# Transposing each expert tile on VectorE in two operations of 1024 columns instead of four of 512

## The chip, the core and the metric

One core of a Trainium2 chip runs the whole program. The metric is the time of one execution in microseconds (us), as the device measures it. The engines of the core run side by side, each with its own instruction stream, and meet at semaphores: TensorE (PE, with PEld for its weight loads), VectorE (DVE), ScalarE (ACT), GpSimd (POOL) and SyncE (SP), which here only starts transfers from HBM.

## What is computed

One transformer-like layer over 256 tokens of width 2048: a mixing part (projections, gated linear attention and retention, output projection, layer norm), and then an expert part. The change lies in the expert part alone, whose first half is this, cut from the reference:

```python
q = (xt @ w_q).reshape(t, PEER_HEADS, 2, PEER_QDIM // 2)
scores = jnp.einsum('thpd,hpkd->thpk', q, subkeys)
vals, idx = lax.top_k(scores, PEER_TOPK)          # then 16 of the 16 x 16 sums, and a softmax of them
...
act = gelu(einsum('tkd,td->tk', u_tab[eb], xb))   # u_tab: 16384 experts x 2048
out = einsum('tk,tkd->td', gates * act, v_tab[eb])
```

The kernel doesn't gather the rows of `u_tab`. It multiplies all 16384 experts with all tokens, applies the gelu, and weights the result by a matrix that holds the gates of the chosen experts and zero elsewhere. Products of float32 are made from two parts of each operand, an upper and a lower one in a rounded 32-bit format, so that each tile of `u_tab` needs an upper part, a lower part, and two matmuls.

## The kernel before

**The U stage.** `u_tab` is taken in 128 tiles of 128 experts by 2048 columns (1 MB each). A tile must be turned, so that its columns lie on the partitions. It is loaded so that transposing blocks of 32 by 32 is enough. A tile is worked in four quarters of 512 columns, and each quarter goes through four engines:

- SyncE loads the tile into a buffer `u_raw` with four transfers (`load_u`, L341). There are two such buffers, three for tiles 6 to 47. A load waits until `ut_done` tells that the last tile in its buffer is wholly transposed.
- VectorE transposes a quarter from `u_raw` into one of the six slots of the ring `u_t` (L907, in `u_quarter`). It waits until the transfer has landed (`u_in`, at the first quarter) and until TensorE has finished the quarter that lay in the slot six quarters earlier (`uparts_free`).
- ScalarE copies the quarter to its upper part `u_hi` (L547), after `ut_done`.
- GpSimd subtracts and gives the lower part `u_lo` (L1201), after `uhi_done`.
- TensorE waits for `ulo_done` and runs eight matmuls in four pairs: `u_hi` with 512 columns (L1469) and `u_lo` with 256 (L1470). Then it counts `uparts_free` up.

`u_hi` and `u_lo` lie in rings of the same six slots. `slot(j, f)` is `(4 * j + f) % 6`: quarter `f` of tile `j`, tiles counted in sixes. Quarters are numbered 0 to 511 below; the quarter `n` needs the slot of `n - 6`.

**What else VectorE does between the quarters.** Its order is written out by hand. For every tile two behind, `u_add` (L995) adds two halves of the sum before the gelu. In tiles 0 to 23 pieces of the search for the best keys are put behind the second and the fourth quarter (`route_best`, two tiles of three; its stage 3 is L929 and L933, in tiles 4 and 16). In tiles 25 to 50 come the pieces of `route_pick`, one for each tile. From tile 64 on, each tile also has `spread` (L1044), `weigh` (L1052), `hot_rows` (L1030) and `hot_cols` (L1036, four operations), in `u_spread_tile`. `hot_rows` and `hot_cols` make the two operands of four products (L1451) that TensorE runs behind the first quarter of the same tile, once `hot_done` tells of them.

**Behind the U stage** the same scheme runs with the table V, where nothing is transposed: TensorE's matmuls are L1509, and VectorE makes the lower parts (L1090, L1094).

Of the kernel before, what the change touches and what calls it, by code (L numbers as in the profile page):

```python
# [53 lines left out]
U_TWO = 48  # L54
# [39 lines left out]
def build(nc, x, w_in, w_up, b_gate, gla_g, ret_g, w_out, ln1_g, ln1_b, w_q, subkeys, peer_u, peer_v,  # L94
          ln2_g, ln2_b, keep_c, mix_c, out):
    ctx = ExitStack()
    with ctx:
# [6 lines left out]
        def at(name, off, shape, dt=F32):  # L104
            return nc.alloc_sbuf_tensor_at(name, shape, dt, offset=base + off)
# [51 lines left out]
        u_raw = [at(f"u_raw{s}", off, [P, 4 * COL]) for s, off in enumerate((WRK, WRK + 8 * K, BIG + 64 * K))]  # L157
        u_t = at("u_t", WRK + 16 * K, [P, UR, 4 * P])
# [63 lines left out]
        def slot(j, f):  # L222
            return (4 * j + f) % UR
# [20 lines left out]
        ut_done, uhi_done, ulo_done, uparts_free, gelu_done, gelu_free = (  # L244
            sem(n) for n in ("ut_done", "uhi_done", "ulo_done", "uparts_free", "gelu_done", "gelu_free"))
# [420 lines left out]
        def _(dve):  # L666
# [226 lines left out]

            def u_quarter(ii, j, f, three=False):
                s = j % 3 if three else j % 2
                if f == 0:
                    if three:
                        before = 2 * (ii - 1) + j // 3 + 3 * (s < 2)  # L900
                    elif isinstance(ii, int) and ii == 0:
                        before = j // 2
                    else:
                        before = (ii - U_TWO // 6) * 3 + j // 2 + 3 + (U_TWO - 6) // 3
                    dve.wait_ge(u_in[s], before * 64 + 64)
                dve.wait_ge(uparts_free, ii * 24 + 4 * j + f + 1)
                dve.transpose(u_t[:, slot(j, f), :].rearrange("p (f b l) -> p b f l", f=4, b=4),  # L907
                              u_raw[s][:].rearrange("p (b f l) -> p b f l", b=4, l=32)[:, :, 4 * f:4 * f + 4, :]).then_inc(ut_done, 1)


            def route_best(stage, part):
# [38 lines left out]
            def route_split():  # L950


                dve.drain()
                dve.tensor_copy(gmax[:], tops[:, :, 0])
                dve.tensor_copy(idx_f[:].rearrange("p a h s k -> p (a h s k)"), idx_u[:].rearrange("p a r k -> p (a r k)"))
                dve.tensor_scalar(sel_ab[:, 0], sel_u[:], 4, None, ALU.logical_shift_right)
                dve.tensor_scalar(sel_ab[:, 1], sel_u[:], 15, None, ALU.bitwise_and)
                dve.drain()
                dve.tensor_tensor(tops[:], tops[:], gmax[:].unsqueeze(2).to_broadcast([P, TT * PH, TOPK]), ALU.subtract).then_inc(soft_d, 1)
                dve.tensor_copy(sel_f[:], sel_ab[:])  # L960

            def route_pick(s, a, stage, part):

                h0 = 4 * part
                p4 = pick.rearrange("p (h k) a -> p h k a", h=4)
                dve.drain()
                if stage == 0:
                    dve.wait_ge(iota_done, 1)
                    dve.tensor_tensor(pick, iota_ps[:, 0:TOPK].unsqueeze(1).to_broadcast([P, 4 * TOPK, TOPK]),
                                      sel_f[:, s, a * PH + h0:a * PH + h0 + 4].rearrange("p n k -> p (n k)").unsqueeze(2).to_broadcast([P, 4 * TOPK, TOPK]),  # L970
                                      ALU.is_equal)
                elif stage == 1:
                    dve.tensor_tensor(p4, p4, idx_f[:, a, h0:h0 + 4, s, :].unsqueeze(2).to_broadcast([P, 4, TOPK, TOPK]), ALU.mult)
                else:
                    dve.tensor_reduce(ijg[:, s, a, h0 * TOPK:(h0 + 4) * TOPK], pick, AX.X, ALU.add).then_inc(ijg_done, 1)

            def route_gates():
                dve.wait_ge(soft_e, 1)
                dve.drain()
                dve.tensor_reduce(gmax[:], tops[:], AX.X, ALU.add)  # L980
                dve.drain()
                dve.reciprocal(rstd[:], gmax[:])
                dve.drain()
                dve.tensor_tensor(ijg[:, 2].rearrange("p a (h k) -> p (a h) k", k=TOPK), tops[:],
                                  rstd[:].unsqueeze(2).to_broadcast([P, TT * PH, TOPK]), ALU.mult).then_inc(ijg_done, 1)
# [5 lines left out]
            def u_add(ii, j, late=0):  # L991

                dve.wait_ge(cross_done, ii * 6 + j + 1)
                z = u_bank(j)[:, 0:T]
                dve.tensor_tensor(z, z, cross_sb[late][:], ALU.add).then_inc(u_sum, 1)  # L995

            for i in range(U_TURN // 6 * 6):
                for f in range(4):
                    u_quarter(i // 6, i % 6, f, three=6 <= i < U_TWO)
                    if i > 1 and f == 2:  # L1000
                        u_add(i // 6, i % 6 - 2)
                    if i < 24 and i % 3 < 2 and f % 2:
                        n = i // 3 * 2 + i % 3
                        route_best(n % 8, 4 * (f // 2) + 2 + n // 8)
                    elif U_PICK <= i and f == 1:
                        n = i - U_PICK
                        route_pick(n // 12, n // 6 % 2, n % 3, n // 3 % 2)
                if i == 24:
                    route_split()
                elif i == 30:  # L1010
                    route_gates()
            route_pick(1, 1, 2, 1)
            with dve.Fori(U_TURN // 6, U_SPREAD // 6) as ii:
                for j in range(6):
                    for f in range(4):
                        u_quarter(ii, j, f)
                        if f == 2:
                            u_add(ii, j - 2, 1)
            for i in range(U_SPREAD // 6 * 6, U_SPREAD):
                for f in range(4):  # L1020
                    u_quarter(i // 6, i % 6, f)
                    if f == 2:
                        u_add(i // 6, i % 6 - 2, 1)


            def hot_rows(q):

                if not isinstance(q, int) or q:
                    dve.wait_ge(spread_mm, q)
                dve.tensor_tensor(hot_j[:], iota.unsqueeze(1).to_broadcast([P, 4, P]),  # L1030
                                  bank(4)[:, bass.ds(T + q * 4, 4)].unsqueeze(2).to_broadcast([P, 4, P]), ALU.is_equal)

            def hot_cols(q):
                for k in range(4):
                    t = bass.ds(q * 4 + k, 1)
                    ins = dve.tensor_scalar(hot_i[:, k, :], iota_ps, pick_ig[:, 0, t], pick_ig[:, 1, t], ALU.is_equal, ALU.mult)  # L1036
                ins.then_inc(hot_done, 1)

            def spread(q, r):

                dve.drain()
                dve.wait_ge(spread_mm, q + 1)
                g4 = act_w[:, :, bass.ds(q, 1)].rearrange("p h q i t -> p h (q i) t")
                dve.tensor_tensor(g4, g4, bank(2 + r).rearrange("p (t h i) -> p h i t", t=4, h=2), ALU.mult).then_inc(spread_free, 1)  # L1044

            def weigh(ii, j):

                i = ii * 6 + j
                dve.drain()
                dve.wait_ge(gelu_done, i + 1)  # L1050
                w = tile_w(1, i - P // 2)
                dve.tensor_tensor(w, w, by_four(u_bank(j)[:, 0:T]), ALU.mult).then_inc(gelu_free, 1)  # L1052

            def u_spread_tile(ii, j, spreads=True, weighs=True):
                q = ii * 6 + j - U_SPREAD
                u_quarter(ii, j, 0)
                if spreads:
                    spread(q - 2, j % 2)
                u_quarter(ii, j, 1)
                if weighs:  # L1060
                    weigh(ii, j - 3)
                u_quarter(ii, j, 2)
                u_add(ii, j - 2, 1)
                hot_rows(q)
                u_quarter(ii, j, 3)
                hot_cols(q)

            dve.wait_ge(ijg_sb, 1)
            for i in range(U_SPREAD, U_UNROLL):
                if i == U_SPREAD + 2:  # L1070
                    dve.wait_ge(ones_done, 16)
                    dve.wait_ge(gelu_done, U_SPREAD)
                u_spread_tile(i // 6, i % 6, spreads=i > U_SPREAD + 1, weighs=i > U_SPREAD + 2)
            with dve.Fori(U_UNROLL // 6, P // 6) as ii:
                for j in range(6):
                    u_spread_tile(ii, j)
            for j in range(2):
                u_spread_tile(P // 6, j)
# [491 lines left out]
```

## Time and profile before

| | us |
|---|---|
| median of 3 runs | 2061.8 |
| the runs | 2057.56, 2061.80, 2062.09 |
| profiled execution | 2061.78 |
| its span in the profile | 2060.0 |
| TensorE busy | 2028.4 |
| VectorE busy | 1231.1 |
| ScalarE busy | 970.8 |
| GpSimd busy | 1089.0 |

The span is the time from the first instruction to the last; 1.8 us of the profiled execution lie around it. The U stage runs from about 569 us (first matmul of L1469) to about 1348 us. The times in the rows below are counted from the span's start.

### The profile page before, as it was taken

To read this page: it belongs to the slowest core of one execution; us is meant where nothing else is said; L and a number is where in the kernel's file an instruction comes from. 1 tells how busy PE (TensorE), PEld (TensorE's weight loads), DVE (VectorE), ACT (ScalarE), POOL (GpSimd) and SP (SyncE) were. 2 spreads that over 40 slices of the span, in tenths; PEclk is the share of its full clock that TensorE was granted. 3 is DMA by queue.
4 is the path that set the end of the run, shared out by engine and by line. 5 is a ranking of instruction groups with operands and counts; after the bars stand their busy time and mean duration, and the time that the engine had idled before them with its cause. 6 is when DMAs were issued, how large, how long until landed. Compare 5 with 4: busy or idle time off the path is not lost.

```text
span 2060.0 us, 34135 instructions
## 1 busy us (share of the span) xinstructions
PE 2028.4 (98%) x11230; PEld 1763.3 (86%) x11230; DVE 1231.1 (60%) x2147; ACT 970.8 (47%) x1436; POOL 1089.0 (53%) x699
## 2 busy tenths in 40 slices
PE   8999999999999999999999999999999999999997
PEld 8998888878988888888888888888888888888885
DVE  1753121123878877658899999955555555555557
ACT  4544334444455566574444444444444444444442
POOL 6877778886778998898777777700000000000000
PEclk9999999999999999999999999999999999999998
DMA  8555657576678887676666666665555555555553
GB/s 281 174 153 167 195 176 248 179 201 170 166 170 192 192 190 186 163 185 164 164 163 163 163 163 163 164 262 186 199 188 196 191 192 195 189 198 186 201 185 140
DMA packets 149282, 381.29 MB, mean 185 GB/s; under 512 B 15568, under 2 KB 18256, under 8 KB 131424
## 3 DMA queue, kind: packets, MB, share of 16 engines
q1 hardware_dynamic: 149072, 380.27, 64.0%
q8 instruction: 42, 0.69, 0.1%
q14 instruction: 24, 0.20, 0.0%
q10 hardware_dynamic: 144, 0.13, 0.0%
HBM read 376.15 MB, written 4.19 MB: 185 GB/s over the span
## 4 chain that ended last, share of the span: by engine, by line
PE 88%; POOL 5%; issue 4%; DVE 1%; DMA 1%; DVEq 1%; ACT 0%; SPq 0%; POOLq 0%; ACTq 0%
PE ps L1509 33%; PE ps L1469 20%; PE ps L1470 10%; PE ps L1228 6%; PE ps L1230 6%; PE ps L1229 6%; PE ps L1451 3%; POOL w_lo L1162 3%; POOL u_lo L1201 2%; DMA raw<-in_w_in 1%; PE ps L1325 1%; DVEq L655 0%; PE ps L1434 0%; DVE h_again L656 0%; PE ps L1343 0%
## 5 line engine op out<-in xcount | busy, mean ns | idle before, releaser
L1469 PE MATMUL ps<-xT,u_hi 128*128 128x512 f32 x2048 | 727.5, 399 | 0.4 <-POOL u_lo L1201 0.4
L1201 POOL TENSOR_TENSOR u_lo<-u_t,u_hi 128x512 fp32r<-128x512 f32 x512 | 653.1, 1297 | 129.2 <-ACT u_hi L547 126.9
L1470 PE MATMUL ps<-xT,u_lo 128*128 128x256 f32 x2048 | 573.3, 280 | 0.0
L547 ACT ACTIVATE u_hi<-u_t 128x512 fp32r<-128x512 f32 x512 | 321.0, 632 | 359.9 <-DVE u_t L907 358.6
L1162 POOL TENSOR_TENSOR w_lo<-raw,w_hi 128x1024 fp32r<-128x1024 f32 x175 | 427.3, 2457 | 119.1 <-ACT w_hi L404 115.5
L1469 PEld LDWEIGHTS ps<-xT,u_hi 128*128 128x128 f32 x2048 | 384.7, 188 | 90.8 <-POOL u_lo L1201 0.5
L907 DVE STREAM_TRANSPOSE u_t<-u_raw 128x512 f32<-128x512 f32 x512 | 356.4, 703 | 105.5 <-PE ps L1470 75.5
L1470 PEld LDWEIGHTS ps<-xT,u_lo 128*128 128x128 f32 x2048 | 386.7, 189 | 0.0
L1167 POOL TENSOR_TENSOR small<-small 128x1 f32<-128x1 f32 x4 | 2.8, 699 | 707.6 <-DVE small L1122 707.6
L1509 PE MATMUL ps<-v_hi,m_hi 128*128 128x512 f32 x1024 | 316.6, 389 | 0.0
L1509 PE MATMUL ps<-v_lo,m_hi 128*128 128x512 f32 x1024 | 316.6, 389 | 0.0
L1509 PE MATMUL ps<-v_hi,m_lo 128*128 128x512 f32 x1024 | 316.6, 389 | 0.0
L404 ACT ACTIVATE w_hi<-raw 128x1024 fp32r<-128x1024 f32 x175 | 184.7, 1059 | 274.8 <-PE ps L1230 263.7
L1090 DVE TENSOR_TENSOR v_lo<-v_raw,v_hi 128x1024 fp32r<-128x1024 f32 x128 | 156.8, 1225 | 141.8 <-ACT v_hi L622 141.8
L1509 PEld LDWEIGHTS ps<-v_hi,m_lo 128*128 128x128 f32 x1024 | 192.2, 188 | 39.9
L1509 PEld LDWEIGHTS ps<-v_lo,m_hi 128*128 128x128 f32 x1024 | 192.2, 188 | 39.9
L1509 PEld LDWEIGHTS ps<-v_hi,m_hi 128*128 128x128 f32 x1024 | 192.1, 188 | 39.9
L622 ACT ACTIVATE v_hi<-v_raw 128x1024 fp32r<-128x1024 f32 x126 | 133.7, 1061 | 164.6 <-PE ps L1509 148.0
L1228 PE MATMUL ps<-xT,w_hi 128*128 128x256 f32 x640 | 183.9, 287 | 2.3 <-DVE xT L662 1.8
L1094 DVE TENSOR_TENSOR v_lo<-v_raw,v_hi 128x1024 fp32r<-128x1024 f32 x128 | 156.8, 1225 | 48.4 <-ACT v_hi L627 48.4
L1229 PE MATMUL ps<-xT,w_hi 128*128 128x256 f32 x640 | 181.6, 284 | 0.0
L1230 PE MATMUL ps<-xT,w_lo 128*128 128x256 f32 x640 | 181.5, 284 | 0.0
(191 smaller groups left out, 2313.0 us busy)
## 6 DMA issues: line engine op xcount, KB each, us to landing
u_raw<-in_peer_u SPq DMA_DIRECT2D x512, 256.0 KB, 4.8
v_raw<-in_peer_v SPq DMA_DIRECT2D x128, 1024.0 KB, 4.8
raw<-in_w_in SPq DMA_DIRECT2D x111, 512.0 KB, 3.7
raw<-in_w_out SPq DMA_DIRECT2D x32, 512.0 KB, 3.7
raw<-in_w_peer_q SPq DMA_DIRECT2D x128, 128.0 KB, 3.5
x_again<-in_x SPq DMA_DIRECT2D x1, 2048.0 KB, 9.0
h_dram<-o_sb SPq DMA_DIRECT2D x1, 2048.0 KB, 8.4
h_again<-h_dram SPq DMA_DIRECT2D x1, 2048.0 KB, 12.6
```

Source lines behind the costliest of these rows:

```text
L404: act.activation(w_hi[:, k % HI_RING, :], raw[:, k, :], ACT.Copy).then_inc(hi_done, 1)
L547: act.activation(u_hi[:, slot(j, f), :], u_t[:, slot(j, f), :], ACT.Copy).then_inc(uhi_done, 1)
L907: dve.transpose(u_t[:, slot(j, f), :].rearrange("p (f b l) -> p b f l", f=4, b=4), u_raw[s][:].rearrange("p (b f l) -> p b f l", b=4, l=32 ...
L1090: dve.tensor_tensor(v_lo[:, 2 * s, :], v_raw[:, 2 * s, :], vh[0].bitcast(F32), ALU.subtract)
L1162: pool.tensor_tensor(w_lo[:, k, :], raw[:, k, :], w_hi[:, k % HI_RING, :].bitcast(F32), ALU.subtract).then_inc(lo_done, 1)
L1201: pool.tensor_tensor(u_lo[:, r, :], u_t[:, r, :], u_hi[:, r, :].bitcast(F32), ALU.subtract).then_inc(ulo_done, 1)
L1228: pe.matmul(o, lh, rh, start=start, stop=False, skip_group_check=lint)
L1229: pe.matmul(o, lh, rl, start=False, stop=False, skip_group_check=lint)
L1230: return pe.matmul(o, ll, rh, start=False, stop=stop, skip_group_check=lint)
L1469: pe.matmul(acc, u_hi[:, r, c], xT[:, :, kt, :], start=kt == 0, stop=False)
L1470: ins = pe.matmul(acc[:, 0:T], u_lo[:, r, c], xT_hi[:, kt, :], start=False, stop=kt == KT - 1)
L1509: ins = pe.matmul(bank(4 * a + 2 * h + c), m, v[:, c * 512:(c + 1) * 512], start=start and p == 0, stop=stop and p == 2)
```

## The change

The four transposes of a tile become two. `u_quarter` becomes `u_half`: one operation turns 1024 columns (two quarters) into two slots of the ring that lie side by side, and counts `ut_done` up by two. It waits until both slots are free, so for the count of its second quarter. The first half takes the place of quarter 0 in VectorE's order, the second that of quarter 2. ScalarE, GpSimd and TensorE keep their code: they still work quarter by quarter, with the same counts.

```diff
-            def u_quarter(ii, j, f, three=False):
+            def u_half(ii, j, f, three=False):
...
-                dve.wait_ge(uparts_free, ii * 24 + 4 * j + f + 1)
-                dve.transpose(u_t[:, slot(j, f), :].rearrange("p (f b l) -> p b f l", f=4, b=4),
-                              u_raw[s][:].rearrange("p (b f l) -> p b f l", b=4, l=32)[:, :, 4 * f:4 * f + 4, :]).then_inc(ut_done, 1)
+                dve.wait_ge(uparts_free, ii * 24 + 4 * j + f + 2)
+                r = slot(j, f)
+                dve.transpose(u_t[:, r:r + 2, :].rearrange("p f n -> p (f n)").rearrange("p (f b l) -> p b f l", f=8, b=4),
+                              u_raw[s][:].rearrange("p (b f l) -> p b f l", b=4, l=32)[:, :, 4 * f:4 * f + 8, :]).then_inc(ut_done, 2)
...
             for i in range(U_TURN // 6 * 6):
                 for f in range(4):
-                    u_quarter(i // 6, i % 6, f, three=6 <= i < U_TWO)
+                    if f % 2 == 0:
+                        u_half(i // 6, i % 6, f, three=6 <= i < U_TWO)
...
             def u_spread_tile(ii, j, spreads=True, weighs=True):
                 q = ii * 6 + j - U_SPREAD
-                u_quarter(ii, j, 0)
+                u_half(ii, j, 0)
                 if spreads:
                     spread(q - 2, j % 2)
-                u_quarter(ii, j, 1)
                 if weighs:
                     weigh(ii, j - 3)
-                u_quarter(ii, j, 2)
+                u_half(ii, j, 2)
                 u_add(ii, j - 2, 1)
                 hot_rows(q)
-                u_quarter(ii, j, 3)
                 hot_cols(q)
```

VectorE's rows in tile 4, where stage 3 of the search lies between the quarters (`u_raw_95` is the buffer of this tile, `u_raw_96` that of tile 5). Before:

```order
L907 STREAM_TRANSPOSE u_t<-u_raw_95 128x4x4x32 [waits uparts_free,u_in0]
L907 STREAM_TRANSPOSE u_t<-u_raw_95 128x4x4x32 [waits uparts_free]
L929 MAX_INDEX idx_u<-vals,scores 128x8 x4
L933 TENSOR_TENSOR cand<-vals 128x256 x2
L907 STREAM_TRANSPOSE u_t<-u_raw_95 128x4x4x32 [waits uparts_free]
L995 TENSOR_TENSOR ps<-ps,cross_early 128x256 [waits cross_done]
L907 STREAM_TRANSPOSE u_t<-u_raw_95 128x4x4x32 [waits uparts_free]
L929 MAX_INDEX idx_u<-vals,scores 128x8 x4
L933 TENSOR_TENSOR cand<-vals 128x256 x2
L907 STREAM_TRANSPOSE u_t<-u_raw_96 128x4x4x32 [waits uparts_free,u_in1]
```

Now (lines behind L907 are one higher):

```order
L908 STREAM_TRANSPOSE u_t<-u_raw_95 128x4x8x32 [waits uparts_free,u_in0]
L930 MAX_INDEX idx_u<-vals,scores 128x8 x4
L934 TENSOR_TENSOR cand<-vals 128x256 x2
L908 STREAM_TRANSPOSE u_t<-u_raw_95 128x4x8x32 [waits uparts_free]
L996 TENSOR_TENSOR ps<-ps,cross_early 128x256 [waits cross_done]
L930 MAX_INDEX idx_u<-vals,scores 128x8 x4
L934 TENSOR_TENSOR cand<-vals 128x256 x2
L908 STREAM_TRANSPOSE u_t<-u_raw_96 128x4x8x32 [waits uparts_free,u_in1]
```

The fourth quarter has moved ahead of `u_add`, and the first quarter of tile 5 is no longer ready before its second.

VectorE's rows at the end of a tile from 64 on, between its third quarter and `hot_cols`. Before:

```order
L907 STREAM_TRANSPOSE u_t<-u_raw_96 128x4x4x32 [waits uparts_free]
L993 REGISTER_ALU
L995 TENSOR_TENSOR ps<-ps,cross_late 128x256 [waits cross_done]
L1029 REGISTER_ALU
L1030 ISA [waits spread_mm]
L1030 TENSOR_TENSOR hot_j<-keepc,ps 128x512
L906 REGISTER_ALU
L907 STREAM_TRANSPOSE u_t<-u_raw_96 128x4x4x32 [waits uparts_free]
L1036 ISA
L1036 TENSOR_SCALAR hot_i<-ps,pick_ig 128x128
```

Now:

```order
L908 STREAM_TRANSPOSE u_t<-u_raw_96 128x4x8x32 [waits uparts_free]
L994 REGISTER_ALU
L996 TENSOR_TENSOR ps<-ps,cross_late 128x256 [waits cross_done]
L1033 REGISTER_ALU
L1034 ISA [waits spread_mm]
L1034 TENSOR_TENSOR hot_j<-keepc,ps 128x512
L1040 ISA
L1040 TENSOR_SCALAR hot_i<-ps,pick_ig 128x128
```

The wait for the slot of quarter 3 now stands ahead of `u_add` and `hot_rows`, which before ran while VectorE would have waited for that slot.

## Rows read from the trace of the kernel before

**Rows 1.** The page: busy time by engine, and TensorE's share in 40 slices.

```profile
PE 2028.4 (98%) x11230; PEld 1763.3 (86%) x11230; DVE 1231.1 (60%) x2147; ACT 970.8 (47%) x1436; POOL 1089.0 (53%) x699
...
PE   8999999999999999999999999999999999999997
```

**Rows 2.** The page's groups: line engine operation xcount | busy us, mean ns | idle before.

```profile
L1469 PE MATMUL ps<-xT,u_hi 128*128 128x512 f32 x2048 | 727.5, 399 | 0.4 <-POOL u_lo L1201 0.4
L1201 POOL TENSOR_TENSOR u_lo<-u_t,u_hi 128x512 fp32r<-128x512 f32 x512 | 653.1, 1297 | 129.2 <-ACT u_hi L547 126.9
...
L907 DVE STREAM_TRANSPOSE u_t<-u_raw 128x512 f32<-128x512 f32 x512 | 356.4, 703 | 105.5 <-PE ps L1470 75.5
...
L1090 DVE TENSOR_TENSOR v_lo<-v_raw,v_hi 128x1024 fp32r<-128x1024 f32 x128 | 156.8, 1225 | 141.8 <-ACT v_hi L622 141.8
```

**Rows 3.** Window 668 to 930: length, TensorE busy (instructions), clock, DMA share, GB/s.

```profile
668.00:930.00 262.00, 262.00 (x1487) 1.00 0.77 183
```

**Rows 4.** Timeline, TensorE, 595 to 668: start us, us, engine, line, operation.

```profile
595.70 0.40 PE L1469 MATMUL ps<-xT,u_hi 128*128 128x512 f32 x1
...
598.47 0.40 PE L1469 MATMUL ps<-xT,u_hi 128*128 128x512 f32 x1
...
599.15 0.47 PE L1469 MATMUL ps<-xT,u_hi 128*128 128x512 f32 x1 [0.17 <-POOL u_lo L1201]
...
600.63 0.40 PE L1469 MATMUL ps<-xT,u_hi 128*128 128x512 f32 x1
...
606.30 0.40 PE L1469 MATMUL ps<-xT,u_hi 128*128 128x512 f32 x1
...
666.72 0.40 PE L1469 MATMUL ps<-xT,u_hi 128*128 128x512 f32 x1
...
667.43 0.50 PE L1469 MATMUL ps<-xT,u_hi 128*128 128x512 f32 x1 [0.20 <-POOL u_lo L1201]
```

**Rows 5.** Timeline, VectorE, tiles 4 and 5, and tile 17's first quarters.

```profile
587.32 1.32 DVE L907 STREAM_TRANSPOSE u_t<-u_raw 128x512 f32<-128x512 f32 x2 [0.49 <-DMA u_raw<-in_peer_u]
...
591.74 0.70 DVE L907 STREAM_TRANSPOSE u_t<-u_raw 128x512 f32<-128x512 f32 x1
...
594.67 1.67 DVE L933 TENSOR_TENSOR cand<-vals 128x256 f32<-128x256 f32 x2
596.27 1.88 DVE L907 STREAM_TRANSPOSE u_t<-u_raw 128x512 f32<-128x512 f32 x3
...
664.64 1.88 DVE L907 STREAM_TRANSPOSE u_t<-u_raw 128x512 f32<-128x512 f32 x3
```

**Rows 6.** Timeline, ScalarE and GpSimd, tile 5.

```profile
597.00 1.23 ACT L547 ACTIVATE u_hi<-u_t 128x512 fp32r<-128x512 f32 x2 [2.70 <-DVE u_t L907]
...
597.71 5.06 POOL L1201 TENSOR_TENSOR u_lo<-u_t,u_hi 128x512 fp32r<-128x512 f32 x4 [1.98 <-ACT u_hi L547]
```

**Rows 7.** Timeline, tiles 59 and 60: VectorE, then GpSimd, then TensorE.

```profile
903.00 0.71 DVE L907 STREAM_TRANSPOSE u_t<-u_raw 128x512 f32<-128x512 f32 x1 [0.33 <-PE ps L1470]
905.64 1.31 DVE L907 STREAM_TRANSPOSE u_t<-u_raw 128x512 f32<-128x512 f32 x2 [1.92 <-DMA u_raw<-in_peer_u]
...
901.49 5.06 POOL L1201 TENSOR_TENSOR u_lo<-u_t,u_hi 128x512 fp32r<-128x512 f32 x4 [0.58 <-ACT u_hi L547]
...
905.63 0.40 PE L1469 MATMUL ps<-xT,u_hi 128*128 128x512 f32 x1
```

**Rows 8.** Timeline, tiles 66 and 67: VectorE, then TensorE.

```profile
944.24 0.71 DVE L907 STREAM_TRANSPOSE u_t<-u_raw 128x512 f32<-128x512 f32 x1 [0.48 <-PE ps L1470]
944.87 1.32 DVE L1036 TENSOR_SCALAR hot_i<-ps,pick_ig 128x128 f32<-128x128 f32 x4
...
949.27 0.40 DVE L995 TENSOR_TENSOR ps<-ps,cross_late 128x256 f32<-128x256 f32 x1
949.58 0.67 DVE L1030 TENSOR_TENSOR hot_j<-keepc,ps 128x512 f32<-128x512 f32 x1
...
948.20 1.05 PE L1451 MATMUL ps<-hot_i,hot_j 128*128 128x128 f32 x8
```

More of the change, by code:

```diff
@@ L1015, in _ @@
                     for f in range(4):
-                        u_quarter(ii, j, f)
+                        if f % 2 == 0:
+                            u_half(ii, j, f)
                         if f == 2:
@@ L1020, in _ @@
                 for f in range(4):
-                    u_quarter(i // 6, i % 6, f)
+                    if f % 2 == 0:
+                        u_half(i // 6, i % 6, f)
                     if f == 2:
```

## The prediction

> **What bounds the kernel now.** I read the page first. TensorE is busy 98% of the span and its digits stand at 9 in every slice behind the first, while VectorE has 60% [rows 1]. So a saving on VectorE counts only where TensorE is waiting for it. The groups of the page say how often that is in the U stage: before its 2048 matmuls of L1469 TensorE was idle for 0.4 us in all, and GpSimd's `u_lo` ended that [rows 2]. A window over tiles 17 to 63 shows it busy all the time at the full clock, 2.4 GHz [rows 3]. "Busy" hides a short wait, because the ends of matmuls are modelled, so I then went by the starts. A pair (L1469 and L1470) takes 0.346 us between 595.70 and 598.47 (eight pairs in 2.77 us). The start at 599.15 comes 0.68 us after the one before it, so TensorE lost 0.33 us there; the start at 667.43 comes 0.71 us after 666.72, a loss of 0.36 us against the 0.354 us of that stretch [rows 4]. Both times the profile names GpSimd. They are the first quarters of tile 5 (number 20) and tile 17 (number 68). These 0.7 us are all that the U stage loses to its feed, out of some 780 us.
>
> **Why it waits in those two places.** The chain to a quarter is transpose, upper part, lower part, matmuls, and the ring of six slots lets it run up to six quarters ahead. In tiles 4 and 16 the search puts some 3 us of other work between transposes, twice. In tile 4 the transposes start at 587.32 (two), 591.74, and, for quarter 20, at 596.27, right behind L933 [rows 5]. ScalarE takes quarter 20 at 597.00, GpSimd at 597.71 [rows 6], and with 1.30 us for the lower part [rows 2] it is ready at 599.01, when TensorE has run dry. Tile 17 repeats this from 664.64 on [rows 5].
>
> **What the change removes, adds and moves.**
>
> *The transpose itself.* Before, 512 operations of 0.703 us, less their overlap: two in a row take 1.32 us [rows 2, 5]. The trace has no transpose of 1024 columns. From above it is bounded by two of 512 in a row, 1.32 us. From below by the nearest VectorE operation of 1024 columns, L1090 with 1.225 us [rows 2]. I take 1.24 us: L1090 is the row of the same length, and one operation should not cost more than that class by much. VectorE then saves 0.08 us a pair, or 256 x 0.08 = 20 us of its busy time. None of it lies on the path, except in the two waits above, so it is worth 0.7 us at the very most.
>
> For the same term the Trainium skill (Vector Engine (DVE) Microarchitecture Reference, section 5.2) gives 1.0417 ns a column plus about 75 ns an instruction; by that, as an estimate, a merged pair would take 1.14 us and the saving would be 46 us of VectorE's time. The sum for the kernel would be the same, since what hides it is TensorE's own work. The Trainium skill (VectorE: DVE Perf Modes, section on the TRN2 errata) advises few large tiles because the latency is exposed between instructions; no row here shows VectorE's throughput as the bound, so I give that advice no weight against what follows.
>
> *The first quarter of a pair comes out later.* It now waits for the second quarter's slot too, and for the whole operation: 1.24 us instead of 0.70. In the two dry places I count it through. Tile 4's first pair must wait for the slot of quarter 17, which comes free when TensorE starts quarter 12: without its stall TensorE would have started quarter 20 at 598.82 (599.15 less 0.33), and quarter 12 eight steps of 4 x 0.346 us before, 587.75. The wait of VectorE ends about 0.2 us behind such a start. So the pair begins at 587.95 instead of 587.32, ends 0.55 us later than before, and the search behind it moves by as much. In front of the second piece the pair 18, 19 and `u_add` save some 0.1 us. The search therefore ends at 596.7, against 596.27. Then the pair 20, 21 ends at 597.95, where quarter 20 alone ended at 596.97. GpSimd starts and ends some 0.95 us later, and TensorE starts quarter 20 at 600.1 instead of 599.15: **+0.9 us**. In tile 17 the same pattern of instructions gives the same shift, since TensorE too is 0.9 us later by then, and with it the slots: **+0.9 us** again.
>
> Below, this is bounded by 0.54 us each (the longer operation alone), above by 1.95 us each (a whole quarter less in the ring, 1.41 us, plus 0.54). So the term is +1.8 us, between +1.1 and +3.9.
>
> *The usual tile.* In tiles 59 and 60 GpSimd has the first quarter of tile 59 ready at 902.8 (901.49 plus 1.29), and TensorE starts it at 905.63: a margin of 2.8 us [rows 7]. The change takes 0.5 to 1.4 us of it. GpSimd is the tightest of the helpers, with 4 x 1.27 us in a tile of 5.66 us, and has 0.58 us idle ahead of each tile [rows 7]. Its idle time moves but need not grow. Cost: nothing. What hides it is the ring; without that cover each tile would lose up to 0.54 us.
>
> *The transfers.* SyncE's next load waits for the whole tile to be transposed. The last pair starts where quarter 3 started, for the same slot (903.00 in tile 59), and ends 0.53 us later. The next tile's pair would be later by that at its transfer, but it waits for quarter 1's slot anyway, which before was served 0.65 us behind quarter 0. VectorE's 1.9 us of idle time before 905.64 is such a wait for a transfer [rows 7]. Cost: nothing, out of the same 2.8 us.
>
> *From tile 64 on.* `hot_cols` now stands behind the pair, `u_add` and `hot_rows`, all of which wait for the slot of quarter 3. In tile 66 that slot came at 944.24, `hot_cols` ended at 946.19, and TensorE began the four products at 948.20: a margin of 2.0 us [rows 8]. Now it ends at 944.24 + 1.24 + 0.31 (949.27 to 949.58) + 0.67 + 1.32 = 947.78. That leaves **0.4 us**, and I count nothing, but this is the thinnest cover that the change leaves, and 64 tiles stand behind it.
>
> **The sum.** 2061.78 (the profiled execution; it equals the median to 0.02 us, so nothing is added for the difference) + 1.8 = **2063.6 us**.
>
> **The rivals.**
>
> 1. *The pitch after a wait.* After the stall at 599.15 the pairs come every 0.354 us (sixteen pairs from 600.63 to 606.30), before it every 0.346 us [rows 4]. The clock is the same. So TensorE falls into one of at least two rhythms when it starts again after a wait, and in this run both restarts led into the slow one. Other start times may lead into the fast one. Between tiles 17 and 50 there are 34 x 16 = 544 pairs, worth 544 x 0.008 = 4.3 us; with tiles 5 to 16 and 51 to 63 it is 7.2 us. Against it: two of two restarts in the trace were slow. For it: the same trace shows the fast one in the same code, and one of the three runs of before took 4.2 us less than the others. Time: 2059.3, down to 2056.4.
>
> 2. *More dry places.* Tiles 4 and 16 are not the only ones where VectorE does other work. If each further heavy tile starts a quarter poorer, up to three more of them (pieces of the search, and the one-time work behind tiles 24 and 30) run dry, at 0.9 to 1.95 us each: 2064.5 to 2069.4. Against it: the whole window from 668 to 930 shows no idle TensorE today [rows 3].
>
> 3. *Slower, in the last 64 tiles.* TensorE waits for `hot_done`. It decides at 0.4 us: were the operation, or a wait of `u_add` for ScalarE, longer by more than that, each of 64 tiles would lose the excess. With 0.6 us too much it is 64 x 0.2 = 12.8 us, or 2076.4. For it: the margin is a fifth of what it was. Against it: all the terms are from rows of this very stretch, and `u_add` waited for nothing there.
>
> 4. *VectorE's saved time reaches the path.* The dry places come because VectorE is late, and each pair gives back 0.08 us or more. Then both stalls go: 2061.1. Against it: a pair gives its first quarter 0.54 us later, which is far more than it saves.
>
> That the change isn't made as it says is ruled out: VectorE's rows show one transpose where two stood.
>
> **Chances and range.** The forecast 0.50, rival 1 0.27, rival 2 0.12, rival 3 0.05, rival 4 0.06. A measurement of this kernel tells a change from none at about 0.3%, here 6.2 us, so "same" is 2055.6 to 2068.0. The forecast, nearly all of rivals 1 and 4 and two thirds of rival 2 lie in it: 0.87. Faster 0.04, the far end of rival 1; slower 0.09, the end of rival 2 and rival 3. The range leaves out rival 3 and both far ends: 2057.0 to 2067.5.
>
> **What the next profile would show.** VectorE: 256 transposes of 128x1024 near 1.24 us, its busy time near 1210 us. TensorE: the starts of quarters 20 and 68 each some 0.9 us later than one pair behind the start before, beyond today's stall; nothing of that kind elsewhere up to tile 63. The four products of L1451 start on time, some 0.4 us after `hot_cols` ends. The pitch behind the two restarts tells rival 1 from the forecast. Wrong I would be if VectorE's pair took well over 1.32 us, if TensorE's digits fell below 9 in the U stage, or if a stage without transposes changed its length.

## The result and the profile after

| | before | changed |
|---|---|---|
| median, us | 2059.41 (7 runs) | 2067.37 (7 runs) |
| lowest and highest | 2057.56, 2062.09 | 2065.93, 2069.47 |
| profiled execution, its span | 2061.78, 2060.0 | 2067.37, 2064.5 |
| first to last matmul of L1469 (now L1471) | 569.2 to 1348.0 | 569.4 to 1352.5 |

The ratio is 1.0038, with an interval of 1.0029 to 1.0047. The change makes the kernel slower, by 8.0 us. The forecast was 2063.6 us, 1.8 us over the profiled execution of before, and 0.87 had been put on "within 0.3%". The time lies inside the range, 0.1 us from its upper end; the ratio, 1.0038, lies outside the 0.3%.

The page after, against [rows 1, 2]: VectorE has 20 us less to do, just as worked out, and TensorE waits ten times as long before `u_lo`. The columns of a group are those of [rows 2].

```profile
span 2064.5 us, 33942 instructions
...
PE 2029.8 (98%) x11230; PEld 1766.5 (86%) x11230; DVE 1211.3 (59%) x1891; ACT 945.9 (46%) x1436; POOL 1086.8 (53%) x699
...
L1471 PE MATMUL ps<-xT,u_hi 128*128 128x512 f32 x2048 | 727.2, 399 | 4.5 <-POOL u_lo L1203 4.3
...
L908 DVE STREAM_TRANSPOSE u_t<-u_raw 128x1024 f32<-128x1024 f32 x256 | 317.6, 1241 | 134.1 <-PE ps L1472 110.9
```

A transpose of 1024 columns takes 1.241 us. The idle time of L1471 was 0.4 us [rows 2] and is 4.5. 4.3 us of it are three waits, of quarters 20, 68 and 100 (TensorE's timeline after, as [rows 4]):

```profile
601.47 0.47 PE L1471 MATMUL ps<-xT,u_hi 128*128 128x512 f32 x1 [1.88 <-POOL u_lo L1203]
...
671.73 0.63 PE L1471 MATMUL ps<-xT,u_hi 128*128 128x512 f32 x1 [1.78 <-POOL u_lo L1203]
...
718.59 0.50 PE L1471 MATMUL ps<-xT,u_hi 128*128 128x512 f32 x1 [0.64 <-POOL u_lo L1203]
```

From start to start, less the 0.35 us of a pair, TensorE loses 2.05, 1.95 and 0.80 us there. Two more waits are too short for the idle column: quarters 18 and 66 start 0.60 and 0.64 us behind the start before them, a loss of 0.25 and 0.29. Together 5.3 us, against 0.7 before.

How VectorE fares in tiles 4 and 5 after (to be laid beside [rows 5]), and GpSimd below it:

```profile
588.25 1.25 DVE L908 STREAM_TRANSPOSE u_t<-u_raw 128x1024 f32<-128x1024 f32 x1 [0.29 <-DMA u_raw<-in_peer_u]
...
590.92 2.32 DVE L934 TENSOR_TENSOR cand<-vals 128x256 f32<-128x256 f32 x2
593.17 1.23 DVE L908 STREAM_TRANSPOSE u_t<-u_raw 128x1024 f32<-128x1024 f32 x1
594.33 0.40 DVE L996 TENSOR_TENSOR ps<-ps,cross_early 128x256 f32<-128x256 f32 x1
...
596.04 2.12 DVE L934 TENSOR_TENSOR cand<-vals 128x256 f32<-128x256 f32 x2
598.08 2.36 DVE L908 STREAM_TRANSPOSE u_t<-u_raw 128x1024 f32<-128x1024 f32 x2
```

```profile
590.24 2.73 POOL L1203 TENSOR_TENSOR u_lo<-u_t,u_hi 128x512 fp32r<-128x512 f32 x2 [0.27 <-ACT u_hi L547]
595.14 2.73 POOL L1203 TENSOR_TENSOR u_lo<-u_t,u_hi 128x512 fp32r<-128x512 f32 x2 [2.18 <-ACT u_hi L547]
600.05 2.52 POOL L1203 TENSOR_TENSOR u_lo<-u_t,u_hi 128x512 fp32r<-128x512 f32 x2 [2.18 <-ACT u_hi L547]
```

The two sums of a piece take 2.32 and 2.12 us, where before they took 1.86 and 1.67 (the second is the 1.67 of [rows 5]). Each time GpSimd is at work on the two quarters of the pair just turned, and its two operations take 2.73 us instead of the 2.52 of the pair at 600.05, beside which no sums run. Taken one by one, the four sums of tile 4 took 0.43, 1.52, 1.34 and 0.41 us before, so in each piece one of the two met GpSimd; after, they take 0.89, 1.51, 0.69 and 1.51 us, so both do.

Behind quarter 68 something else shows. Windows after, VectorE to GpSimd left in (columns: TensorE, weight loads, VectorE, ScalarE and GpSimd busy, then granted clock, DMA share, GB/s):

```profile
671.73:675.40 3.67, 3.67 (x12) 3.08 (x13) 1.74 (x3) 2.11 (x5) 3.67 (x4) 0.54 0.83 209
```

For 3.7 us the granted clock is 0.54, so near the lower of TensorE's two levels, 1.2 GHz. The clock was at full speed up to a wait of 1.95 us; 4.9 us earlier there had been a wait of 0.29 us. A pair takes 0.64 us there, which costs 1.6 us more.

**Where the 8.0 us are.** In the two traces: more waiting 4.65 us (5.34 less 0.69), the low clock 1.6 us, and a pace of TensorE that is faster in tiles 18 to 24 and 51 to 63 than in the profile before (0.347 us a pair against 0.353), some 2 us back (more on this below). That is 4.3 us, and the spans differ by 4.5. Another 1.1 us lie outside the spans (2.87 against 1.78 us; the other six runs of the changed kernel have 1.8 to 3.0), and 2.4 us come from the profile of before, which lay that much over the median of its seven runs. So the profile before was a poor stand-in for the median: the sum was made against 2061.78 and the result is told against 2059.41. Of the 8.0 us only the waiting is nearly the same from execution to execution (4.65 us here, 4.3 us between the two later executions at the end of the next section). The rest varies, and no run divides it further.

### The profile page after: what moved, and what is told of

It is laid out like the page before. It is cut to its first block, busy times and chain, and to the rows that moved or that the text cites. A ratio compares the mean times of both kernels' runs of the same rounds, so it can differ in the third digit from the quotient of the medians.

```text
span 2064.5 us, 33942 instructions
## 1 busy us (share of the span) xinstructions
PE 2029.8 (98%) x11230; PEld 1766.5 (86%) x11230; DVE 1211.3 (59%) x1891; ACT 945.9 (46%) x1436; POOL 1086.8 (53%) x699
## 4 chain that ended last, share of the span: by engine, by line
PE 84%; POOL 7%; issue 5%; DVE 1%; DMA 1%; DVEq 1%; ACT 0%; POOLq 0%; SPq 0%; ACTq 0%
PE ps L1511 33%; PE ps L1471 21%; PE ps L1472 10%; POOL w_lo L1164 5%; PE ps L1230 5%; PE ps L1232 5%; PE ps L1231 5%; PE ps L1453 3%; POOL u_lo L1203 2%; DMA raw<-in_w_in 1%; PE ps L1327 1%; DVEq L655 0%; DVE h_again L656 0%; PE ps L1345 0%; ACT w_hi L404 0%
## 5 line engine op out<-in xcount | busy, mean ns | idle before, releaser
L1471 PE MATMUL ps<-xT,u_hi 128*128 128x512 f32 x2048 | 727.2, 399 | 4.5 <-POOL u_lo L1203 4.3
L547 ACT ACTIVATE u_hi<-u_t 128x512 fp32r<-128x512 f32 x512 | 295.1, 624 | 391.5 <-DVE u_t L908 391.1
L1471 PEld LDWEIGHTS ps<-xT,u_hi 128*128 128x128 f32 x2048 | 385.2, 188 | 94.4 <-POOL u_lo L1203 3.9
L908 DVE STREAM_TRANSPOSE u_t<-u_raw 128x1024 f32<-128x1024 f32 x256 | 317.6, 1241 | 134.1 <-PE ps L1472 110.9
```

The lines of the kernel that those rows point to most:

```text
L547: act.activation(u_hi[:, slot(j, f), :], u_t[:, slot(j, f), :], ACT.Copy).then_inc(uhi_done, 1)
L908: dve.transpose(u_t[:, r:r + 2, :].rearrange("p f n -> p (f n)").rearrange("p (f b l) -> p b f l", f=8, b=4), u_raw[s][:].rearrange("p (b ...
L1471: pe.matmul(acc, u_hi[:, r, c], xT[:, :, kt, :], start=kt == 0, stop=False)
```

## The experiments

All times are medians of 6 to 11 executions where nothing else is said, each with the kernel before run beside it on the same chip. Beside the first four runs its median was 2061.76 us, beside the next four 2059.66, beside the last four 2060.53; a ratio always belongs to the kernel before. Theory A: the loss arises only where VectorE does other work between transposes, tiles 4, 5, 16, 17 and 24. Theory B: every tile pays a little for the merged operation.

**Halves from tile 25 on.**

```diff
-                    if f % 2 == 0:
+                    if i < 25:
+                        u_quarter(i // 6, i % 6, f, three=6 <= i < U_TWO)
+                    elif f % 2 == 0:
                         u_half(i // 6, i % 6, f, three=6 <= i < U_TWO)
```

> Quarters of 512 columns in tiles 0 to 24 (the search), halves of 1024 from tile 25 on. Theory A (the loss is made only where the search stands between the transposes, tiles 4, 5, 16, 17, and behind tile 24): the starts of quarters 20 and 68 lose some 0.3 us each as before, GpSimd is late at most at quarter 100, by up to 0.8 us, and the time is within 3 us of before. Theory B (every tile pays a little for the pair, by transfers, ports or the pace of TensorE): 80% of the 8 us stays, so 6 us over before.

Measured: 2059.68 us, ratio 1.0001 (0.9991 to 1.0011). The waits are those of the kernel before, and there is none at quarter 100:

```profile
600.54 0.47 PE L1488 MATMUL ps<-xT,u_hi 128*128 128x512 f32 x1 [0.16 <-POOL u_lo L1220]
...
668.82 0.50 PE L1488 MATMUL ps<-xT,u_hi 128*128 128x512 f32 x1 [0.21 <-POOL u_lo L1220]
```

So 103 tiles in halves cost nothing that can be measured, the last 64 of them with the thin margin of `hot_done`.

**Halves in tiles 0 to 25 alone.**

```diff
-                    u_quarter(i // 6, i % 6, f, three=6 <= i < U_TWO)
+                    if i > 25:
+                        u_quarter(i // 6, i % 6, f, three=6 <= i < U_TWO)
+                    elif f % 2 == 0:
+                        u_half(i // 6, i % 6, f, three=6 <= i < U_TWO)
```

> The other part alone: halves in tiles 0 to 25, quarters of 512 from tile 26 on. Theory A: all the waits of the changed kernel are here again (0.3 and 2.0 us at quarters 18 and 20, 0.3 and 2.0 at 66 and 68, a slow clock for some 4 us behind the last, 0.8 at quarter 100), and the time is 5 to 9 us over before. Theory B: 20% of the 8 us, under 2 us over before.

Measured: 2067.81 us, ratio 1.0035 (1.0022 to 1.0048). All the waits are back:

```profile
602.30 0.47 PE L1488 MATMUL ps<-xT,u_hi 128*128 128x512 f32 x1 [1.86 <-POOL u_lo L1220]
...
671.84 0.50 PE L1488 MATMUL ps<-xT,u_hi 128*128 128x512 f32 x1 [1.79 <-POOL u_lo L1220]
```

From start to start it loses 0.23 and 2.03 us at quarters 18 and 20, 0.80 and 1.96 at 66 and 68, and 0.80 at 100. The low clock is here again too, behind the same quarter 68: 0.56 from 673.2 to 677.0 us, and it sets in 1.3 us after TensorE has started again. The two runs split the change in two parts (tile 25 is in both), and one part has the whole loss. Theory B is out.

**The sums without two SBUF operands, in the kernel before and in the changed one.** In tiles 4 and 16 the two sums of each piece are replaced by four operations that read PSUM and one SBUF operand. Half of the candidate sums are thereby left out, so these kernels serve for times alone. The diff is shortened: the condition that keeps the old sums everywhere else is not shown.

```diff
-                    for n in sums:
-                        h = n % PH
-                        dve.tensor_tensor(cand[:, n, :]..., v[:, h, 0, :]..., v[:, h, 1, :]..., ALU.add)
+                    for n in sums:
+                        for to in (cand[:, n, :], bank(3)[:, 2 * P * (n % 2):2 * P * (n % 2) + 2 * P]):
+                            dve.tensor_tensor(to..., bank(2)[:, 0:2 * P]..., v[:, n % PH, 1, :]..., ALU.add)
```

> The kernel before, where stage 3 of the search in tiles 4 and 16 makes four VectorE operations that read PSUM and one SBUF operand, in the place of its two sums with both operands in SBUF; the candidate sums of half the heads are left out, so only times are read. Theory C (a VectorE operation with two SBUF operands waits for GpSimd's): the four take about 1.4 us in each place, the same everywhere, whatever GpSimd does, against 1.7 to 2.2 us for two before; TensorE then waits for nothing at quarters 20 and 68. Rival D (the long sums are long because of their broadcast operands): the new ones, which keep one broadcast operand, take over 2 us as well and vary.

> The changed kernel with the same exchange of stage 3 in tiles 4 and 16 (the candidate sums of half the heads are left out). Theory C: the four operations take 1.4 us here too, the lower part of quarter 20 is ready some 0.9 us later than in the kernel before with the same exchange, which is what the prediction counted for the ring alone, and TensorE loses 0.4 to 0.8 us at quarter 20 in the place of 2.3 at quarters 18 and 20. Rival E (the ring alone makes the whole loss, the sums only look longer): quarter 20 is ready 1.9 us later than in the other kernel, and TensorE loses 1.3 us or more.

Measured: 2054.83 and 2062.67 us, one run each. VectorE at the first piece of tile 4, in the kernel before with the exchange, then in the changed one with it:

```profile
589.76 0.43 DVE L933 TENSOR_TENSOR cand<-ps,vals 128x256 f32<-128x256 f32 x1
590.10 0.42 DVE L933 TENSOR_TENSOR ps<-ps,vals 128x256 f32<-128x256 f32 x1
590.43 0.41 DVE L933 TENSOR_TENSOR cand<-ps,vals 128x256 f32<-128x256 f32 x1
590.76 0.42 DVE L933 TENSOR_TENSOR ps<-ps,vals 128x256 f32<-128x256 f32 x1
```

```profile
591.70 0.43 DVE L934 TENSOR_TENSOR cand<-ps,vals 128x256 f32<-128x256 f32 x1
592.04 0.42 DVE L934 TENSOR_TENSOR ps<-ps,vals 128x256 f32<-128x256 f32 x1
592.37 0.41 DVE L934 TENSOR_TENSOR cand<-ps,vals 128x256 f32<-128x256 f32 x1
592.70 0.42 DVE L934 TENSOR_TENSOR ps<-ps,vals 128x256 f32<-128x256 f32 x1
```

Each takes 0.41 to 0.43 us, all sixteen operations of either kernel, with the same number of columns and one broadcast operand kept, while GpSimd works on. The real sums take 0.41 us where GpSimd is idle and up to 1.52 where it isn't. So rival D falls: the time depends on what the operands are and on GpSimd. The Trainium skill has a rule for this (SBUF — State Buffer, section "SBUF: two separate sides"): VectorE operations with two SBUF inputs and GpSimd operations that read SBUF share a port pair, and the one that starts first holds it to its end. The traces agree: in the kernel before a sum that starts at 590.29, beside a GpSimd operation that ends at 591.53, ends only at 591.81; a GpSimd operation that meets a sum grows from 1.29 us to as much as 1.5; and no transpose of 1024 columns, with its one input, takes more than 1.25 us.

With this exchange the lower part of quarter 20 was in time in the kernel before (ready at 598.11, started at 598.63). In the changed one TensorE waited:

```profile
596.80 2.56 POOL L1206 TENSOR_TENSOR u_lo<-u_t,u_hi 128x512 fp32r<-128x512 f32 x2 [1.71 <-ACT u_hi L547]
...
598.63 0.39 PE L1474 MATMUL ps<-xT,u_hi 128*128 128x512 f32 x1
```

```profile
599.22 2.54 POOL L1208 TENSOR_TENSOR u_lo<-u_t,u_hi 128x512 fp32r<-128x512 f32 x2 [1.66 <-ACT u_hi L547]
...
600.65 0.48 PE L1476 MATMUL ps<-xT,u_hi 128*128 128x512 f32 x1 [0.66 <-POOL u_lo L1208]
```

TensorE lost 0.83 us (1.18 from start to start). Quarter 20 is later by 0.83 + 0.52 - 0.15 (the least time seen between the end of the lower part and the first matmul here) = 1.2 us. With the real sums it is 2.05 + 0.25 - 0.33 = 2.0 us. So 1.2 us of the shift belong to the ring and the long operation, where 0.95 had been worked out, and 0.8 us to the sums. At quarter 68, where the least time seen is 0.05 us, the same account gives 0.43 + 0.51 - 0.05 = 0.9 us for the ring and the long operation, of 1.9 in all, and so 1.0 us for the sums. The numbers of theory C hold but for the last: the loss is 0.83, just over its 0.4 to 0.8.

The exchange does not bring the two kernels together: the changed one takes 7.8 us more, in one execution of each. It loses 0.83, 0.43 and 0.64 us at quarters 20, 68 and 100. Behind quarter 20, up to tile 50, it also runs at 0.353 us a pair, where the other, which waits nowhere there, keeps 0.347: 4.9 us more. So a short wait can cost more by the pace behind it than by its own length.

**Pairs of 512-column transposes.** The wait for both slots is kept, the operation is not merged.

```diff
                 dve.wait_ge(uparts_free, ii * 24 + 4 * j + f + 2)
-                r = slot(j, f)
-                dve.transpose(u_t[:, r:r + 2, :]..., u_raw[s]...[:, :, 4 * f:4 * f + 8, :]).then_inc(ut_done, 2)
+                for h in (f, f + 1):
+                    dve.transpose(u_t[:, slot(j, h), :]..., u_raw[s]...[:, :, 4 * h:4 * h + 4, :]).then_inc(ut_done, 1)
```

> Four transposes of 512 columns as before, but issued in pairs behind the changed kernel's wait for both slots. Theory F (the loss comes from pairing: the wait for two slots, the two quarters that reach ScalarE and GpSimd close together, and the longer sums that this gives): most of the loss is here too; the sums of stage 3 take over 2 us a pair, quarters 18 and 66 come within 0.5 us of the wait, TensorE loses 1.2 to 2.0 us at quarter 20 and at 68, against 2.3 and 2.2, and the time is 3 to 8 us over before. Theory G (it is the length of the one operation, 1.24 us, that holds the first quarter back): the loss at quarter 20 falls to under 0.9 us, near the 0.3 us of before, and the time is within 2 us of before.

Measured: 2063.24 us, ratio 1.0013 (1.0003 to 1.0023).

```profile
591.38 1.86 DVE L934 TENSOR_TENSOR cand<-vals 128x256 f32<-128x256 f32 x2
...
596.09 1.70 DVE L934 TENSOR_TENSOR cand<-vals 128x256 f32<-128x256 f32 x2
...
600.58 0.48 PE L1471 MATMUL ps<-xT,u_hi 128*128 128x512 f32 x1 [0.83 <-POOL u_lo L1203]
```

Neither theory had it. Quarter 20 costs 1.00 us and quarter 68 1.01, between what the two had named, and the sums are no longer than before. So the wait for both slots costs about 0.7 us in each place. The rest, another 1.3 us in tiles 4 and 5, comes only when the two are one operation. It fits 0.54 us because the first quarter comes with the second, and 0.8 us because GpSimd then starts its two operations right where the sums begin; 0.7 and 0.54 together are the 1.2 us found above. My expectation that pairing by itself lengthens the sums was wrong.

**The search moved, first try.** The second piece of each odd stage goes to the next tile, which had none, behind its second quarter; the one-time work behind tile 24 (`route_split`) is cut in two.

```diff
-                    if i < 24 and i % 3 < 2 and f % 2:
-                        n = i // 3 * 2 + i % 3
-                        route_best(n % 8, 4 * (f // 2) + 2 + n // 8)
+                    if i < 24 and (f % 2 if i % 3 == 0 else f == 1):
+                        n, a = i // 3 * 2 + (i % 3 > 0), f // 2 if i % 3 == 0 else i % 3 - 1
+                        route_best(n % 8, 4 * a + 2 + n // 8)
+                    elif i == 24 and f == 1:
+                        route_split(0)
```

> The kernel before (quarters), with the second piece of every odd stage of the search moved from the fourth quarter of its tile to the second quarter of the next tile, which had none, and with the one-time work behind tile 24 in two pieces. Theory A: VectorE is away for one stage 3 piece at a time, no quarter up to tile 50 is waited for, TensorE stays in the pace of 0.346 us a pair from tile 1 to tile 50, the U stage takes 771 to 773 us, and the time is 2053 to 2057 us. Rival (the pace changes by itself, not at waits): the pace of 0.354 us shows up between tiles 5 and 50 though nothing is waited for.

> The changed kernel (halves) with the same two moves. Theory A: without the two pieces in one tile the halves are in time too, TensorE waits nowhere for more than 0.3 us, and the time is that of the other kernel with the moves within 2 us. Theory B (a cost of the halves apart from the search): it stays 4 us or more slower than that kernel.

Measured: 2060.32 us, ratio 1.0006 (0.9996 to 1.0016), and 2062.93 us, ratio 1.0019 (1.0009 to 1.0028). Quarter 20 is in time in the first, with 1.8 us to spare, but quarter 28 isn't:

```profile
607.37 1.31 DVE L907 STREAM_TRANSPOSE u_t<-u_raw 128x512 f32<-128x512 f32 x2 [2.85 <-DMA u_raw<-in_peer_u]
...
610.17 0.50 PE L1472 MATMUL ps<-xT,u_hi 128*128 128x512 f32 x1 [0.28 <-POOL u_lo L1204]
```

Tile 5 now holds its buffer for longer, to 600.07 us; tile 7's load starts at 600.09, and VectorE waits 2.85 us for that transfer. The wait has moved, and nothing is gained. The halves wait at quarters 18, 22, 66, 70 and 98, and stay 2.6 us over the quarters, between what the two theories had named (2 and 4 us).

**The search moved, second try.** The piece now stands behind the fourth quarter, when the tile's buffer has been given back. The condition is `f in ((1, 3), (1,), (3,))[i % 3]`; the rest is as above.

> As the kernel before with moved search, but the second piece of an odd stage now stands behind the fourth quarter of the next tile, so that this tile is transposed, and its buffer given back to the transfers, before it. Theory A: neither quarter 20 nor 68 nor 28 is waited for, TensorE keeps 0.346 us a pair from tile 1 to tile 50, the U stage takes 771 to 773 us, and the time is 2 to 6 us under before, so about 2055 us. Rival: a wait comes up elsewhere (the first quarters of tile 6 or 7), the pace falls to 0.354 us behind it, and the time is that of before within 2 us.

> The changed kernel with the same places of the search. Theory A: the losses at quarters 20 and 68 fall from 2 us to under 0.5 us each, TensorE's clock stays at full speed, and the time is within 3 us of the other kernel with these places, 2056 to 2060 us. Theory B (the halves cost something by themselves): it stays 5 us or more over that kernel.

Measured: 2055.72 us, ratio 0.9980 (0.9971 to 0.9989), and 2060.95 us, ratio 1.0001 (0.9992 to 1.0010). The first beats both kernels. Windows from 576.5 to 850 us, with TensorE alone (busy, instructions, clock, DMA share, GB/s): before, changed, changed once more, quarters with the search apart, halves with the search apart.

```profile
576.50:850.00 273.50, 273.13 (x1548) 1.00 0.79 184
```

```profile
576.50:850.00 273.50, 268.98 (x1516) 0.99 0.77 180
```

```profile
576.50:850.00 273.50, 269.16 (x1523) 1.00 0.77 181
```

```profile
576.50:850.00 273.50, 273.50 (x1582) 1.00 0.83 188
```

```profile
576.50:850.00 273.50, 272.68 (x1545) 1.00 0.79 184
```

In the same 273.5 us the fourth kernel does 34 matmuls more than before, although before TensorE lost only 0.7 us there, which is four matmuls. The other 30 come from its pace: 0.3467 us a pair in all the tiles 1 to 63. The halves with the search apart still wait at quarters 18, 24, 66, 72 and 98, 1.6 us in all, and run at 0.353 us a pair from quarter 24 to 71 and from 98 to 203, some 4 us more, so that they stay 5.2 us over the quarters. That is over the 3 us that I had given theory A, and by that number theory B had it ("5 us or more"). The trace doesn't bear theory B out: the waits again stand only in tiles of the search and in tile 24, which has half of the one-time work, and the slow pace begins at two of them. But it shows that moving the search doesn't make the halves free.

**Halves in all but six tiles.** Tiles 4, 5, 16, 17, 24 and 25 keep quarters (`if i in (4, 5, 16, 17, 24, 25)` in the place of `if i < 25`).

> Halves in all tiles but 4, 5, 16, 17, 24 and 25, which keep quarters of 512 columns. Theory A: with quarters in these six tiles alone the loss at quarters 18, 20, 66, 68 and 100 is gone but for some 0.3 to 0.8 us at 20 and 68, and the time is within 3 us of before. Theory B: 122 of 128 tiles are in halves, so nearly all of the 8 us stays.

Measured: 2063.09 us, ratio 1.0009 (0.9999 to 1.0018). The time is within the 3 us of theory A. A miss in part: quarters 20 and 68 cost 1.24 and 1.45 us, not 0.3 to 0.8.

```profile
600.82 0.47 PE L1488 MATMUL ps<-xT,u_hi 128*128 128x512 f32 x1 [1.08 <-POOL u_lo L1220]
...
670.24 0.49 PE L1488 MATMUL ps<-xT,u_hi 128*128 128x512 f32 x1 [1.28 <-POOL u_lo L1220]
```

The margin at quarter 16, ahead of the first piece, is 2.3 us here and 3.2 in the kernel before. The halves of tile 3 hand the ring over with less in it, so the loss is made partly before the heavy tile.

**Both kernels once more.**

> The kernel before once more, for the pace of TensorE. If the pace behind the waits at quarters 20 and 68 is a matter of the moment at which TensorE starts again, another execution of the same program may show 0.346 us a pair where the first showed 0.354; with the slow pace in both places the U stage takes 778.8 us, with the fast one behind quarter 68 some 773.5 us. If the pace belongs to the program, it is 0.354 us again in all the tiles from 5 to 63.

> The changed kernel once more, for TensorE's clock and pace. The waits at quarters 18, 20, 66, 68 and 100 depend on the order of the work alone and come back within 0.1 us (quarter 20 some 2.4 us behind the start before it, quarter 68 some 2.3). The low clock behind quarter 68 (0.54 for 3.7 us) comes back if it belongs to the wait; the pace between the waits may differ.

Measured: 2061.62 and 2067.29 us, one run each. The waits come back within 0.15 us: in the kernel before 0.68 and 0.72 us at quarters 20 and 68 from start to start, and a new one of 0.49 at quarter 32; in the changed kernel 0.57, 2.39, 0.67, 2.28 and 1.00 at 18, 20, 66, 68 and 100. The pace differs: before, tiles 5 to 7 now run at 0.347 us, and it falls to 0.353 at quarter 32; the changed kernel stays at 0.353 from quarter 20 on. The low clock does not come back:

```profile
672.22 0.50 PE L1471 MATMUL ps<-xT,u_hi 128*128 128x512 f32 x1 [1.77 <-POOL u_lo L1203]
672.55 0.28 PE L1472 MATMUL ps<-xT,u_lo 128*128 128x256 f32 x1
672.67 0.40 PE L1471 MATMUL ps<-xT,u_hi 128*128 128x512 f32 x1
```

## Why the prediction was right, and where it was not

- **The transpose**: 1.24 us taken, 1.241 measured; VectorE's busy time 1211 us, with "near 1210" expected. The bounds were 1.22 and 1.32.
- **The place and the sign**: the search at quarters 20 and 68. Right, and the two halves of the change show it: all the loss with halves in tiles 0 to 25, none with halves from 25 on.
- **The size, the step that was too small**: "+0.9 us" in each place measured 1.97 us (2.05 + 0.25 - 0.33) and 1.88 us (1.95 + 0.29 - 0.36). The step was "the search behind it moves by as much": it carried the length of the sums over from [rows 5]. They grew by 0.46 and 0.45 us in tile 4 because GpSimd's work now falls on both of them, where before it fell on one. The ring alone was nearly right, 1.2 us against 0.95, as the pair of kernels with other sums shows. My upper bound of 1.95 us for each place was passed by 0.02 us in the first and nearly reached in the second. The lateness also shows at the quarter two earlier, 18 and 66, where no wait had been named.
- **Rival 2**, more dry places, came in part, at one place: quarter 100, 0.80 us, behind tile 24. There the second of the two shifts (L957 before, L958 after) takes 1.38 us instead of 0.28, again while GpSimd is busy; no run takes this cause apart. It had been given 0.12 by itself, not as an addition to the forecast.
- **The usual tile, the transfers**: no wait in any other tile, as forecast.
- **`hot_done`**: a margin of 0.4 us forecast. `hot_cols` ends at 952.27 after and the products begin at 952.82, so 0.55 us, and TensorE does not wait. From tile 64 to the last it takes 414.1 us in both kernels, so rival 3 is out. The lines for `hot_cols` and the products:

```profile
950.92 1.35 DVE L1040 TENSOR_SCALAR hot_i<-ps,pick_ig 128x128 f32<-128x128 f32 x4
...
952.82 1.05 PE L1453 MATMUL ps<-hot_i,hot_j 128*128 128x128 f32 x8
```

- **Rival 1**, the pace, was real but was no case of its own: it goes both ways in every kernel. It is worth some 6 us in the U stage, more than any term of the sum. The kernels with no waits up to tile 50 (other sums, and the search apart) have a U stage of 771.7 and 771.6 us against 778.8, of which waits are 0.7. The prediction's 0.008 us a pair was 0.0066 over whole tiles, and its 7.2 us for all of them should have been 7.5 by its own numbers.
- **The low clock** was not forecast at all: 1.6 us in the profiled execution, absent in the other, and there again with halves in tiles 0 to 25 alone.
- **Luck**: the direction of each wait was right, but a rise of 8.0 us was met by a forecast of 1.8. That 2067.37 lies in the range owes 2.4 us to the profiled execution that the sum started from. Counted from the median of seven, 2059.41, the same upper end would be 2065.1 us, and the result is 2.3 us above it.
- **The chances**: 0.87 on "within 0.3%" was too sure. The sum had no room for two effects that grow with a wait, and it started 2.4 us above the median that it was later held against. The ratio's interval begins at 1.0029, so the change is most likely over 0.3%, "slower", to which 0.09 had been given. None of the variants with halves beat the kernel before beyond the interval of its ratio.

## What to carry to other kernels

Where a ring feeds the bounding engine, an operation that is merged from two takes one step from the ring and makes its first consumer wait for the whole operation; look for the places where the producer is away longest, since only these pay. Before carrying a duration over to a new order, ask whether it was measured beside an idle or a busy neighbour. If a producer has long pieces of other work, put them apart and behind the point at which it gives its input buffer back: here that was worth 0.2%, more than any change to the transposes.

## What the runs showed of the hardware

- TensorE has two paces for the same pair of matmuls at the same granted clock, 0.3467 and 0.3533 us over whole tiles. In the fourteen traces the pace changed only where TensorE had waited, had run other products in between, or came to a quarter whose lower part was ready no more than 0.15 us ahead (quarter 70 in the first try with the search moved is such a one). Which pace follows did not repeat: behind quarter 68 it was the slow one in both executions of the kernel before and the fast one with halves from tile 25 on, which has the same waits. Why there are two stays open, and no run was made for it.
- A VectorE operation of 256 columns with two SBUF operands took 0.41 us beside an idle GpSimd and up to 1.52 us beside a busy one; with one operand in PSUM it took 0.41 to 0.43 us, beside a busy one too.
- The same wait of 1.9 us at quarter 68 was followed by a granted clock of 0.54 for 3.7 us in one execution of the changed kernel and by full clock in the other; with halves in tiles 0 to 25 alone it was 0.56 for 3.8 us. A wait of 2.0 us at quarter 20 was followed by full clock in all three. What decides it stays open.
